# Where the small products of an RWKV stage are put between the matmuls of a projection

## The reference

```python
zd = z + mu[d] * (shift_seq(z, offset) - z)
r, k, v, lw, la = jnp.split(zd, RWKV_SPLITS, axis=-1)
w_log = -softplus(-(w0[d] + tanh(lw) @ w2[d])) - 0.5          # decay: a small product
a = sigmoid(a0[d] + la @ a2[d])                               # rate: a small product
kk = kk * rsqrt(maximum(sum(kk * kk, axis=-1), 1e-24))        # key norm: a sum over a head
k = k * (1.0 + (a - 1.0) * k_a)
S = S * w + sa[..., :, None] * b + v[..., :, None] * k        # the scan, per token
bonus = merge_dirs(sum(r * k * r_k, axis=-1) * v)             # bonus sum over a head
mean = mean(y); var = mean(square(y - mean))                  # two sums of the readout
return y * (sigmoid(lg) @ g2)                                 # gate of the readout: a small product
```

## Time and profile before

| | before |
|---|---|
| time, median of three | 3369.15 us |
| the profiled execution: span | 3357.8 us |
| TensorE matmul busy | 3114.1 us (93%) |
| VectorE, ScalarE, GpSimd busy | 1500.2, 1162.7, 831.6 us |
| RWKV part of layer 0 | 70 to 895 us |
| RWKV part of layer 1 | 1925 to 2650 us |

### The profile page before, as it was taken

How to read it: one execution, slowest core, us unless ns; L and a number is a source line. 1 busy time by engine, 2 the same in 40 slices (tenths; PEclk the granted TensorE clock), 3 DMA queues, 4 the chain that set the end, 5 groups by cost and what they waited for, 6 DMA issues and landing times.

```text
span 3357.8 us, 79208 instructions
## 1 busy us (share of the span) xinstructions
PE 3114.1 (93%) x34382; PEld 2493.0 (74%) x34382; DVE 1500.2 (45%) x2358; ACT 1162.7 (35%) x2403; POOL 831.6 (25%) x518
## 2 busy tenths in 40 slices
PE   7999898999999998999999888989899989989998
PEld 5777676778777786888888666767667667768886
DVE  4455473745444653100144464756565456330033
ACT  4433333423334424211112353434333345342222
POOL 2211111111123132222223221111111243434453
PEclk9999999999999999999999989999999999999999
DMA  5424242434454441111111233413233343522222
GB/s 212 135 97 145 81 142 101 130 121 144 145 166 151 158 169 57 51 63 62 62 50 63 75 101 98 127 63 120 65 122 106 93 140 115 188 69 95 99 88 75
DMA packets 246714, 364.56 MB, mean 109 GB/s; under 512 B 154080, under 2 KB 155376, under 8 KB 245904
## 3 DMA queue, kind: packets, MB, share of 16 engines
q1 hardware_dynamic: 226976, 294.57, 27.6%
q10 hardware_dynamic: 14976, 35.66, 2.7%
q0 software_dynamic: 4464, 29.92, 2.5%
HBM read 290.88 MB, written 69.21 MB: 107 GB/s over the span
## 4 chain that ended last, share of the span: by engine, by line
PE 76%; DVE 6%; issue 5%; ACT 4%; DMA 2%; DVEq 2%; POOLq 2%; PEld 1%; SPq 1%; POOL 0%; PEldq 0%; ACTq 0%
PE banks L281 20%; PE banks L282 18%; PE banks L283 18%; PE banks L1684 2%; PE banks L1023 2%; PE banks L1695 1%; PE banks L1648 1%; PE banks L395 1%; PE banks L1687 1%; PE banks L1745 1%; POOLq L2430 1%; DVE arena L597 1%; PE banks L2057 1%; PE banks L1051 1%; DMA arena<-chunk_inputs 1%
## 5 line engine op out<-in xcount | busy, mean ns | idle before, releaser
L283 PE MATMUL banks<-hx_rounded,slot_rounded 128*128 128x512 f32 (+1 forms) x1624 | 575.1, 354 | 0.0
L906 POOL TENSOR_TENSOR slot_rounded<-slot,branch_weights_high 128x512 fp32r<-128x512 f32 x188 | 251.4, 1357 | 1286.2 <-ACT branch_weights_high L901 1284.9
L281 PE MATMUL banks<-hx_high,weight_parts 128*128 128x512 f32 (+1 forms) x1512 | 537.9, 356 | 10.9 <-DVE hx_low L545 10.4
L281 PE MATMUL banks<-hx_rounded,branch_weights_high 128*128 128x512 f32 (+1 forms) x1280 | 498.8, 390 | 48.1 <-DVE arena L1364 8.6
L282 PE MATMUL banks<-hx_low,weight_parts 128*128 128x512 f32 (+1 forms) x1512 | 538.0, 356 | 0.0
L283 PE MATMUL banks<-hx_high,weight_parts 128*128 128x512 f32 (+1 forms) x1512 | 535.9, 354 | 0.0
L282 PE MATMUL banks<-resid_rounded,branch_weights_high 128*128 128x512 f32 (+1 forms) x1280 | 452.7, 354 | 0.0
L283 PEld LDWEIGHTS banks<-hx_rounded,slot_rounded 128*128 128x128 f32 x1624 | 312.2, 192 | 44.3
L281 PEld LDWEIGHTS banks<-hx_rounded,branch_weights_high 128*128 128x128 f32 x1280 | 245.9, 192 | 128.2 <-issue 75.6
L281 PEld LDWEIGHTS banks<-hx_high,weight_parts 128*128 128x128 f32 x1512 | 286.6, 190 | 55.1 <-issue 14.3
L283 PEld LDWEIGHTS banks<-hx_high,weight_parts 128*128 128x128 f32 x1512 | 286.3, 189 | 41.1
(11 more groups left out here) (263 smaller groups left out, 5853.7 us busy)
## 6 DMA issues: line engine op xcount, KB each, us to landing
slot<-in_w_mix SPq DMA_DIRECT2D x120, 512.0 KB, 3.9
slot<-in_w_ffn_in SPq DMA_DIRECT2D x88, 512.0 KB, 3.3
arena<-chunk_inputs SPq DMA_DIRECT2D x48, 640.0 KB, 4.5
arena<-in_w_ada SPq DMA_DIRECT2D x50, 512.0 KB, 5.1
slot<-in_w_ffn_out SPq DMA_DIRECT2D x44, 512.0 KB, 3.3
slot<-in_w_ada SPq DMA_DIRECT2D x40, 512.0 KB, 4.3
chunk_inputs<-arena SPq DMA_DIRECT2D x80, 256.0 KB, 3.9
arena<-side_projections POOLq DMA_DIRECT2D x16, 1152.0 KB, 6.1
```

Of the source, the lines that this page charges most:

```text
L281: first = nc.tensor.matmul(out, w_hi, x_hi, start=start, stop=False)
L283: return first, nc.tensor.matmul(out, w_lo, x_hi, start=False, stop=stop)
L906: last = nc.gpsimd.tensor_tensor(slots_r[g % 3][:, half], slots[g % 3][:, half], weights_high(g)[:, half], ALU.subtract)
```

## The change

The generator that mixed tiles and small products is taken apart. `tiles()` gives only tiles, segment 0 always ahead of segment 1 (`tile_order`). `smalls()` gives the small products one by one; `one_small` takes at most one of them at the start of a gap, right behind the chain step and ahead of the tiles' steps, and none when the segment that is being filled has no step left (`left`). A small product goes to the bank that isn't being filled, `1 - filling`. What it costs is added to `filler.spent`. When the next may come is told in gaps after the last (`reach_gap`) in a body, or by the tile reached (`reach`) in the prologue. `place_of` notes the bank for the engine that takes it.

Decay and rate used to come as decay, rate of segment 1 and decay, rate of segment 0, in two banks; now both decays come first and then both rates, and VectorE's scan waits for two sigmoids, not for three. On VectorE r, a and b of a direction are made when their half gap comes, whether or not the bonus sums have been taken: `bonus_taken` does the taking in between, in the gap of each product. Key norms are taken one at a time in their own gaps. ScalarE's threads now stand as preparation, readout, eviction, rounding, and the weights of tile g are rounded when the first segment of tile g - 2 is done. The gate, the two sums and the last bonus addition follow the same pattern. SyncE's order and the chain are as before.

```diff
+                self.filling, self.left = 0, 1
...
+                    banks_of.filling, banks_of.left = tile_bank(l, g, s), KD - 1 - k
...
-            return [0, 1] if (st, t) in ((BODY, 8), (TAIL, 5)) else [1, 0]
+            return [0, 1]
...
             def small(name, s, lhs, rhs, done, taken_by, count=1):
-                at_bank.free(s)
-                nc.tensor.matmul(pair(6)[s], lhs, rhs, start=True, stop=True).then_inc(done.sem, count)
-                at_bank.busy[s] = taken_by
-                mark(name)
-                return COST[s] * 1.25
+                b = 1 - at_bank.filling
+                at_bank.free(b)
+                place = place_of[l, st, hp, name, s] = bank[6 + b][:, 0:SEGS[s][1] - SEGS[s][0]]
+                nc.tensor.matmul(place, lhs, rhs, start=True, stop=True).then_inc(done.sem, count)
+                at_bank.busy[b] = taken_by
+                mark((name, s))
+                last_small[0] = where[0]
+                filler.spent += COST[s] * 1.25
...
+                for n, (x, s) in enumerate(((0, 1), (0, 0), (1, 1), (1, 0))):
+                    r = slice(64 * x, 64 * x + 64)
+                    small(("both", d, x), s, SMALL[r, d * P:(d + 1) * P], LD[r, d, SEGS[s][0]:SEGS[s][1]], pre_prod, (pre_act.sem, pre_act.ready(l, hq, 8 * d + n + 1)))
+                    if n == 3 and d == 1 and st == PRO:
+                        nc.tensor.drain().then_inc(small_free.sem, 1)
+                    yield
...
             def bonus_sum(d):
-                for i, s in enumerate([s for s in sum_order(l, st, d == 0) if s in outs]):
+                for i, s in enumerate(outs):
                     if i == 0:
                         pe.wait_ge(pre_dve.sem, pre_dve.ready(l, hq, 8 * d + 6))
-                    yield small(("bonus", d), s, SAME, TMP[6][:, TSEG[s][0]:TSEG[s][1]], pre_prod, (pre_dve.sem, pre_dve.ready(l, hq, 8 * d + 7 + i)), both_done)
+                    small(("bonus", d), s, SAME, TMP[6][:, TSEG[s][0]:TSEG[s][1]], pre_prod, (pre_dve.sem, pre_dve.ready(l, hq, 8 * d + 7 + i)), both_done)
+                    yield
...
+                    first = 1
+                for t in range(first, TILES_IN[st]):
+                    if (st, t) == (TAIL, 5):
+                        while where[0] < VISITS[TAIL]:
+                            yield None
+                    for s in range(2):
+                        at_tile[0] = (t, s)
+                        yield from tile(t, s)
+
+            def reach(t, s):
+                while at_tile[0] < (t, s) and not last_call[0]:
+                    yield
+
+            def reach_gap(gap):
+                while where[0] < gap and not last_call[0]:
+                    yield
...
+            def smalls():
+                if st == PRO:
+                    yield from reach(2, 0)
                     yield from decay_and_rate(0)
+                    yield from reach(3, 0)
                     yield from key_norm(0)
+                    yield from reach(4, 0)
                     yield from bonus_sum(0)
+                    yield from reach(4, 1)
                     yield from decay_and_rate(1)
+                    yield from reach(5, 1)
                     yield from key_norm(1)
+                    yield from reach(6, 1)
                     yield from bonus_sum(1)
                 elif st == BODY:
                     yield from decay_and_rate(0)
+                    yield from reach_gap(last_small[0] + 2)
                     yield from key_norm(0)
+                    yield from reach_gap(last_small[0] + 5)
                     yield from bonus_sum(0)
+                    yield from reach_gap(last_small[0] + 2)
                     yield from decay_and_rate(1)
+                    yield from reach_gap(last_small[0] + 2)
                     yield from key_norm(1)
+                    yield from reach_gap(last_small[0] + 3)
                     yield from bonus_sum(1)
+                    yield from reach_gap(last_small[0] + 4)
+                if st != PRO:
+                    if st == TAIL:
+                        yield from reach(4, 1)
                     yield from gate_of_readout()
+                    yield from reach_gap(LAST_OF_HEAD + 1 if st == BODY else VISITS[TAIL])
                     yield from sum_of_readout(0)
+                    yield from reach_gap(last_small[0] + 2)
                     yield from sum_of_readout(1)
...
+            def one_small():
+                if at_bank.left:
+                    next(smalls_left, None)
...
             for i in range(FREE[st]):
                 where[0] = i
+                one_small()
                 filler.upto(free * (i + 1) / FREE[st])
...
             filler.upto(1e9)
+            last_call[0] = True
+            for _ in smalls_left:
+                pass
...
-                    yield at((g - 2, 1))
+                    yield at((g - 2, 0 if 0 in tile_segs(l, g - 2) else 1))
                     tile_round(act, l, g)
...
-                    yield at(("both", 1, d)) - 1
+                    yield at((("both", d, 0), 1)) - 1
                     act.preload_act_table_set(SIGMOID)
-                    for i, s in enumerate((1, 0)):
-                        yield at(("both", s, d))
-                        for x, dst, bias in ((0, TMP[3], V_W0), (1, TMP[5], V_A0)):
+                    for x, dst, bias in ((0, TMP[3], V_W0), (1, TMP[5], V_A0)):
+                        for i, s in enumerate((1, 0)):
+                            yield at((("both", d, x), s))
                             if d == 1 and i == 0:
...
-                    yield max(at(("both", 0, d)) + (4 if st == PRO else 2), at(("norm", d)) - 1)
+                    yield max(at((("both", d, 1), 0)) + (4 if st == PRO else 2), at((("norm", d), 1)) - 1)
...
-            threads = [Thread(eviction())] + ([Thread(preparation())] if st != TAIL else []) + ([Thread(readout())] if st != PRO else []) + [Thread(rounding())]
+            threads = ([Thread(preparation())] if st != TAIL else []) + ([Thread(readout())] if st != PRO else []) + [Thread(eviction()), Thread(rounding())]
...
+                    bonus_left = list(enumerate(outs))
+
+                    def bonus_taken(until):
+                        while bonus_left and at((("bonus", d), bonus_left[0][1])) <= until:
+                            i, s = bonus_left.pop(0)
+                            yield max(g, at((("bonus", d), s)))
+                            (c0, c1), (t0, t1) = SEGS[s], TSEG[s]
+                            dst = bonus(hq)[:, c0:c1] if d == 0 else TMP[6][:, c0:c1]
+                            dve.wait_ge(pre_prod.sem, pre_prod.ready(l, hq, k + 7 + i))
+                            nc.vector.tensor_tensor(dst, place_of[l, st, hp, ("bonus", d), s], TMP[2][:, t0:t1], ALU.mult).then_inc(pre_dve.sem, both_done)
...
-                    g = max(g + (1 if st == PRO else 0.5), at(("both", 0, d)) + 1)
+                    g = max(g + (1 if st == PRO else 0.5), at((("both", d, 0), 0)) + 1)
                     yield g
-                    dve.wait_ge(pre_act.sem, pre_act.ready(l, hq, k + 3))
+                    dve.wait_ge(pre_act.sem, pre_act.ready(l, hq, k + 2))
...
-                    assert g < at(("norm", d)), (st, hp, d, g, at(("norm", d)))
-                    g = at(("norm", d))
-                    yield g
-                    for i, s in enumerate(sum_order(l, st)):
+                    assert g < at((("norm", d), 1)), (st, hp, d, g, at((("norm", d), 1)))
+                    for i, s in enumerate((1, 0)):
+                        g = at((("norm", d), s))
+                        yield g
                         dve.wait_ge(pre_prod.sem, pre_prod.ready(l, hq, k + 5 + i))
...
-                    assert g < at(("bonus", d)), (st, hp, d, g, at(("bonus", d)))
-                    g = at(("bonus", d))
-                    yield g
+                    yield from bonus_taken(g + pace)
                     g += pace
                     yield g
                     nc.vector.tensor_tensor(TMP[0][:, tlo:], TMP[0][:, tlo:], TMP[4][:, tlo:], ALU.mult).then_inc(made.sem, 1)
+                    yield from bonus_taken(g + pace)
                     g += pace
                     yield g
                     nc.vector.scalar_tensor_tensor(out=E3, in0=TMP[7], scalar=-1.0, in1=E3, op0=ALU.mult, op1=ALU.mult).then_inc(made.sem, 1)
+                    yield from bonus_taken(g + pace)
                     g += pace
                     nc.vector.tensor_tensor(TMP[5], TMP[5], E2, ALU.mult).then_inc(made.sem, 1)
+                    yield from bonus_taken(999)
+                    g = max(g, at((("bonus", d), outs[-1])))
                 g += pace
                 yield g
+                dve.drain()
                 nc.vector.tensor_tensor(bonus(hq)[:, lo:T], bonus(hq)[:, lo:T], TMP[6][:, lo:T], ALU.add)
...
-                g = at(("sum", 1)) + 1
+                g = at((("sum", 1), outs[-1])) + 1
```

(51 more changed lines are left out.)

69 lines of the change are left out of this document (24 added, 45 removed).

## The result

| | before | after |
|---|---|---|
| time, median | 3369.23 us | 3416.66 us |
| ratio, 95% interval | 1 | 1.0158, 1.0136 to 1.0179 |
| profiled span | 3357.8 us | 3412.0 us |
| TensorE busy | 3114.1 us | 3154.9 us |
| TensorE idle | 243.7 us | 257.1 us |

A forecast was written before the change was run, and what follows sets the result against it. TensorE bounds it, busy 3114.1 of 3357.8 us, so only its idle time and clock can be won. At most 122 us gained against 128 returned, 6 us slower: span 3364, median 3375; own range 3355 to 3395, overall 3318 to 3405.

The forecast's parts named there:

- Ceiling: Most the change could gain: 47 us idle in layer 0, 45 in layer 1, 30 of clock, 122 us.
- Item 1: Small products needed back at once, or paired in one idle bank, in bodies, prologues and tails: 27 us returned.
- Item 2: Block 4's staged load, behind the store of b in SyncE's queue, lands late in six bodies: 29 us returned.
- Item 3: Block 0's load, behind next_tile(4) in SyncE's queue, lands late: 3 us in each of six bodies, 18 us.
- Item 4: Prologue: the second rate's sigmoid waits for b's store, holding the fourth product: 4 us twice, 8 us.
- Item 5: Layer 0: ScalarE stands at tile 5's rounding, delaying square and sigmoid to TensorE's gap 20: 3 us three times, 9 us.
- Item 6: Layer 0: last small product falls to the stage's end, eviction behind it: 1.7 us three times, 5 us.
- Item 7: VectorE does as much work in less time: 0.7 us per layer 0 body, 2 per layer 1 body, 8 us.
- item 8: Lower clock after fifteen stalls of 3 us or more, 4 us at half clock each, at 46%: 28 us returned.
- loads in time: Rival: staged loads nearly in time, so only about 78 us returned; 3325 us, chance 0.33.
- rounding holds the chain: Rival: ScalarE's wait at tile 4's rounding delays the chain's copies, 30 us more; 3405 us, chance 0.17.
- The mark that I set for a wrong forecast: TensorE's waits for staged operands (`chunk_inputs`) under 15 us in all would mean the time of the loads in time rival.

The follow-up runs named there:

- experiment 1: Changed kernel with block 4's staged load issued ahead of the stores in SyncE's body queue: 3380.26 us, ratio 1.0057 to the kernel before.
- experiment 9: experiment 6 with layer 1's bonus sum of direction 0, and small products behind it, one gap sooner in the bodies: 3371.67 us, ratio 1.0035.
- experiment 2: Changed kernel with ScalarE's rounding of tile g put back to the end of tile g-2: 3407.76 us, ratio 1.0131 to the kernel before.
- experiment 5: Kernel before with only the order decay 1, decay 0, rate 1, rate 0, each in its segment's bank: 3380.47 us, ratio 1.0044.
- experiment 6: Changed kernel with block 4's load ahead of the stores, rounding back at the end of tile g-2, and prologues put back: 3348.03 us, ratio 0.9952.
- experiment 3: Changed kernel with its prologue stages alone put back as before, decay still ahead of rate: 3398.45 us, ratio 1.0107 to the kernel before.
- experiment 4: Changed kernel with, in the prologues alone, the bonus sum taken before r, a and b are made: 3412.34 us, ratio 1.0165.

## Why the prediction was wrong

The direction was the forecast's, the size was not: 48 us between the forecast span of 3364 and 3412. I take the sum apart in the same three parts.

*Idle time: the sum was right, its parts much less so.* Ceiling and items without the clock gave -92 + 100 = +8 us; measured +13.4. That these are near each other is in part luck: waits for staged operands, announced as about 20 us in layer 1 and 25 in layer 0, came out as 33.7 and 16.7, and in layer 0 waits of the modulation's rows, of which I had none, filled the place.
- Item 1 (banks, 27 us): small products wait 5.6 us for sigmoids, 5.2 for evictions, 3.1 for norms, and tiles some more; but in layer 0 the rows of the modulation wait another 11.8 us for bonus sums and for the gate's copy (L395: 8.2 and, at L1258, 2.2; L866: 1.4). A row always uses bank 6 and comes while segment 1 fills bank 7; so the "idle" bank isn't idle. I had the rows in the replay and did not follow their bank. The idle time of a body of layer 0 rose by 4.0 us, and the items gave 16.9 - 13.3 = 3.6; but that is two errors that cancel, 3.9 us of these rows that I did not have against 4.3 us less for the loads of items 2 and 3.
- Item 2 (block 4, 29 us for six): 24.1, shown by experiment 1.
- Item 3 (block 0, 18 us for six): 15.8, but 2.0 of it in layer 0 and 13.8 in layer 1. There VectorE makes b late; in experiment 9 placing the bonus sum one gap sooner did not change that.
- Item 4 (prologue, 8 us by b's store): the place was wrong. The store is no wait of note; what came is 11.5 us for the bonus sum's taking. The idle time of both prologues rose by 16 us (8.7 + 0.7 in layer 0, 9.5 - 2.5 in layer 1). The terms gave 4: 12 + 8, less 7 for layer 0 and some 9 us of such waits that before has in layer 1's prologue.
- Item 5 (rounding, 9 us): 10.3, a wait that went with experiment 2's edit; it stood at the row ahead of gap 20. Item 6 (end of a body, 5 us): 6.8 in four waits. Item 7 (VectorE's density, 8 us) shows in no row.

*The clock: the failed step.* Ceiling 30 and item 8's 28 left 2 us of gain; measured 27 us of loss. Fifteen stalls with 4 us at half clock each were too little, and 30 us to be given back too much: the bodies of layer 1 lost 12 us of idle time and yet went from 23.8 to 50.6 us at half clock. I treated every stall alike. In layer 1's bodies of before no wait was longer than 2.5 us, but for the load at their first block; after, 27.3 of the 40.4 us are waits of 3.0 to 5.9 us for staged operands. And in the first prologue half clock went from 13.7 to 37.5 us, while idle time rose by only 8.7. That longer stalls cost more clock for each microsecond is argued from these rows, not shown. For it: without block 4's stalls the time at half clock in these bodies is 25.8 us (experiment 1) and 25.9 (experiment 6). Against it: experiment 5 has 44.4 us there, with no wait over 2.1 us and less idle time than before (first experiment 5, then before):

```profile
2076.80:2572.20 495.40, 445.70 (x8407) 0.96 0.29 91
```

```profile
2066.10:2550.10 484.00, 431.55 (x8407) 0.98 0.30 93
```

What is shown is that in experiment 1 23.6 us less of idle time took 14 us of clock with it.

*The pairs: a term that was missing.* "Everything else (matmuls, sigmoids, table loads, DMAs) is as many as before and hidden as before" was false for decay and rate. Rows 5 could not show it, for the products at 393.41 have 256 columns and run one behind the other; the pair of 512 columns just ahead of them would have. I had this term at nothing. Experiment 5 costs 15 us net; its profile gives the pairs 11.0 us of longer busy time, and the 13.7 us in after are of that size. So the bank that decay and rate no longer wait for was bought with the overlap that they had by standing next to each other.

Of the rivals, the one of loads in time (3325) falls with the L1674 row; "rounding holds the chain" (3405) was nearest in time but not in mechanism: ScalarE's stand held a row, not the chain. The mark that I set for a wrong forecast, waits for `chunk_inputs` under 15 us, was on the fast side only, and the range ended at the rival's 3405 where bounds of the clock term (28 us on either side) should have carried it further.

Still open: what sets the time at half clock where no stall is long, as in experiment 5; why the small products' 23 us of added busy time at full-clock count (111 to 134 us, half of the half-clock time taken off) leave only 13.7 in the whole; and which part of the prologue's layout (the order of the segments, the bank, or the places) carries experiment 3's 17 us, as the one part tried alone, experiment 4, showed no gain.

## What to carry to other kernels

When a product is moved or reordered, look at what stands next to it: here two small matmuls on different halves of the rows, in different banks, ran in the time of one, and an order that is better for the consumer can cost that. Ask of an idle resource who else takes it by name (here the modulation's rows), and follow in each hand-written queue what stands in front of the transfer that gets late: one line there was worth 34 us, twice the 16 us that the best kernel with the new order gained. And give a stall of several microseconds its clock too, in experiment 1 0.6 us for each.

## What the hardware showed

- Matmuls of 64 rows x 512 columns on rows 0 to 63 and 64 to 127, into two banks: starts 7 ns apart, 1.13 us for the two products of two passes each; 1.12 us for one product alone.
- A 64-row product between full-row matmuls delays what follows by 0.19 us against a 128-row one of the same columns (1.39 and 1.20 us to the second matmul behind it).
- The six stores of r, a and b of direction 1 took SyncE 5.93 us to issue in the kernel before (at 498.38), one right behind the other and with no operand waited for. The 5.09 us there and the 7.51 us in after are not such a figure: both hold a wait for b.
